# A hybrid mixer's attention values: values stationary, turned weights moving, two heads side by side

## The reference, cut to what matters

```python
scores = q @ k.T                       # (512, 512), causal
w = softmax(scores)                    # rows sum to one
attn_out[:, head] = w @ v              # (512, 64)
...
return concatenate([attn_out, yg], axis=-1) @ w_out   # 512 + 512 columns -> 1024
```

## Time and profile before

| | |
|---|---|
| median of three runs | 3214.59 us (3209.59, 3214.59, 3214.69) |
| the profiled execution's own time | 3209.03 us |
| its span | 3207.2 us |
| granted TensorE clock | 1.00 all through |
| busy: PE, PEld, DVE, ACT, POOL | 99%, 83%, 57%, 36%, 2% |
| loop iterations 3 to 9 of the first mixer | about 2130 to 2193 us |
| the same of the second mixer | about 2724 to 2787 us |

### The profile page before, as it was taken

The page is one execution under the profiler, slowest core; times in us unless marked ns, Lnnn a source line. Parts: engine busy times, 40 slices in busy tenths (PEclk is TensorE's granted clock), DMA queues, the critical chain, the costliest instruction groups (busy, mean ns, idle before and its releaser), DMA issues.

```text
span 3207.2 us, 36741 instructions
## 1 busy us (share of the span) xinstructions
PE 3190.0 (99%) x15108; PEld 2647.3 (83%) x15108; DVE 1843.9 (57%) x2667; ACT 1157.6 (36%) x1621; POOL 79.6 (2%) x110
## 2 busy tenths in 40 slices
PE   9999999999999999999999999999999999999999
PEld 8888878888888888888888888888788888878887
DVE  6664366666447664367566645987433368763332
ACT  4322254322233222263332223654322245542221
POOL 1000000000000000000000000100000010000000
PEclk9999999999999999999999999999999999999999
DMA  6443322444334443322244433211222322032322
GB/s 187 141 146 111 112 79 88 140 141 141 112 109 131 132 150 116 102 92 79 87 150 145 141 104 98 83 53 53 92 92 93 100 85 78 14 105 92 101 90 73
DMA packets 334252, 339.83 MB, mean 106 GB/s; under 512 B 12422, under 2 KB 329128, under 8 KB 334088
## 3 DMA queue, kind: packets, MB, share of 16 engines
q1 hardware_dynamic: 332128, 333.80, 32.7%
q0 software_dynamic: 1728, 3.62, 0.5%
q10 hardware_dynamic: 232, 0.06, 0.0%
HBM read 335.36 MB, written 2.10 MB: 105 GB/s over the span
## 4 chain that ended last, share of the span: by engine, by line
PE 96%; DVE 2%; ACT 1%; issue 0%; POOL 0%; DVEq 0%; POOLq 0%
PE ps L135 94%; PE ps L138 3%; DVE hl L108 1%; DVE T L108 0%; DVE wl L100 0%; ACT hh L95 0%; DVE x L100 0%; DVE ar L100 0%; DVE T L100 0%; ACT L95 0%; DVE acc L108 0%; DVE acc L100 0%; DVE x L108 0%; ACT ar L95 0%; ACT wh L95 0%
## 5 line engine op out<-in xcount | busy, mean ns | idle before, releaser
L135 PE MATMUL ps<-hh,wl 128*128 128x512 f32 x2760 | 1086.0, 393 | 2.3 <-ACT hh L95 1.5
L135 PE MATMUL ps<-hh,wh 128*128 128x512 f32 x2760 | 1075.4, 390 | 0.0
L135 PE MATMUL ps<-hl,wh 128*128 128x512 f32 x2760 | 1074.3, 389 | 0.0
L100 DVE TENSOR_TENSOR wl<-raw,wh 128x1024 fp32r<-128x1024 f32 (+3 forms) x549 | 654.3, 1193 | 696.2 <-ACT wh L95 695.8
L95 ACT ACTIVATE wh<-raw 128x1024 fp32r<-128x1024 f32 (+3 forms) x549 | 561.2, 1024 | 488.0 <-PE ps L135 487.9
L135 PEld LDWEIGHTS ps<-hh,wl 128*128 128x128 f32 x2760 | 518.2, 188 | 114.0 <-issue 5.9
L135 PEld LDWEIGHTS ps<-hh,wh 128*128 128x128 f32 x2760 | 518.1, 188 | 109.6
L135 PEld LDWEIGHTS ps<-hl,wh 128*128 128x128 f32 x2760 | 518.6, 188 | 104.7 <-issue 0.4
L135 PE MATMUL ps<-uh,wl 128*128 128x512 f32 x1056 | 412.2, 390 | 0.0
L135 PE MATMUL ps<-uh,wh 128*128 128x512 f32 x1056 | 411.1, 389 | 0.0
L135 PE MATMUL ps<-ul,wh 128*128 128x512 f32 x1056 | 410.9, 389 | 0.0
(11 more groups left out here) (239 smaller groups left out, 2668.9 us busy)
## 6 DMA issues: line engine op xcount, KB each, us to landing
raw<-in_ffn_w SPq DMA_DIRECT2D x119, 1024.0 KB, 5.3
raw<-in_w_ada SPq DMA_DIRECT2D x48, 1024.0 KB, 5.2
raw<-in_w_gate_up SPq DMA_DIRECT2D x44, 1024.0 KB, 5.0
raw<-in_m_w_in SPq DMA_DIRECT2D x26, 1024.0 KB, 5.4
raw<-in_w_down SPq DMA_DIRECT2D x16, 1024.0 KB, 5.1
raw<-in_ffn_w SPq DMA_DIRECT2D x16, 768.0 KB, 4.3
raw<-in_w_in SPq DMA_DIRECT2D x12, 1024.0 KB, 5.3
raw<-in_m_w_out SPq DMA_DIRECT2D x8, 1024.0 KB, 5.1
```

What stands on the lines that cost most here:

```text
L100: return self.issue(lambda e: e.tensor_tensor(out, a, b, op))
L135: return self.issue(lambda e: e.matmul(out, l, r, start=start, stop=stop, skip_group_check=True))
```

## The change

Values: heads 2j and 2j+1 are done together in one bank, once in two iterations. 64 columns of v are stationary and a row of PT (512, 384, 256, 128 columns for key block 0 to 3) is moving; head 2j writes partitions 0 to 63 of the bank and head 2j+1 partitions 64 to 127. The result has value columns along the partitions and tokens along the row. TensorE calls `values(j)` in iterations 3, 5, 7 and 9, between the first `between()` and `turn`.

Reciprocals: after the reciprocal DVE copies it, spread over 64 columns, into half of `A(12 + j)`. Behind the values of a pair TensorE transposes that tile (four transposes, one more bank, key `share`), ACT copies the result back to `A(12 + j)` (ahead of its copies for `turn`), and DVE multiplies the bank `val` by it in one 128x512 operation, at the end of its iteration as before.

Behind the loop the 16 transposes are gone; ACT and DVE split `A(12..15)` directly. The order of the parts becomes 0, 1, 4, 2, 5, 3, 6, 7. Two waits of ACT and DVE are changed to the new keys.

```diff
@@ TensorE
-                def values(hd):
-                    b = banks.take((s, "val", hd))
+                def values(j):
+                    heads = (2 * j, 2 * j + 1)
+                    b = banks.take((s, "val", j))
                     pe.wait_ge(*left_of((s, "v", 3)))
-                    for k in (0, 1, 2):
-                        pe.wait_ge(*left_of((s, "pt", hd, k)))
+                    for hd in heads:
+                        for k in (0, 1, 2):
+                            pe.wait_ge(*left_of((s, "pt", hd, k)))
+                    for k in range(4):
+                        for h, hd in enumerate(heads):
+                            done = pe.mm(b[64 * h:64 * h + 64, 128 * k:S], vt[:, k, 64 * hd:64 * hd + 64], PT(hd, k)[:, 0:S - 128 * k],
+                                         k == 0, k == 3)
+                    done.then_inc(formed, (s, "val", j))
+                    b = banks.take((s, "share", j))
+                    pe.wait_ge(worked, (s, "share", 2 * j + 1))
                     for q in range(4):
-                        for k in range(q + 1):
-                            done = pe.mm(b[:, 64 * q:64 * q + 64], PT(hd, k)[:, 128 * (q - k):128 * (q - k) + 128],
-                                         vt[:, k, 64 * hd:64 * hd + 64], k == 0, k == q)
-                    done.then_inc(formed, (s, "val", hd))
+                        done = pe.tr(b[:, 128 * q:128 * q + 128], A(12 + j)[:, 128 * q:128 * q + 128], ident[:, :])
+                    done.then_inc(formed, (s, "share", j))
...
                     between()
+                    if hd > 2 and hd % 2:
+                        values((hd - 3) // 2)
                     if 0 < hd < 9:
                         turn(hd - 1)
                     between()
-                    if hd > 1:
-                        values(hd - 2)
                 while next(ssd, 0):
                     pass
-                for j in range(4):
-                    b = banks.take((s, "cat", j), freed=(lo_part, (s, "c", j)))
-                    pe.wait_ge(*left_of((s, "val", 7)))
-                    for q in range(4):
-                        done = pe.tr(b[:, 128 * q:128 * q + 128], A(12 + q)[:, 128 * j:128 * j + 128], ident[:, :])
-                    done.then_inc(formed, (s, "cat", j))
@@ ACT, in the loop ahead of turn
+                    if hd > 2 and hd % 2:
+                        key = (s, "share", (hd - 3) // 2)
+                        act.wait_ge(formed, key)
+                        act.f(A(12 + (hd - 3) // 2), ps(key)[:, :], ACT.Copy).then_inc(left(key), key)
@@ ACT, behind the loop
-                        act.wait_ge(formed, (s, "cat", j))
-                        part((s, "c", j), ps((s, "cat", j))[:, :], ch[:, j, :])
+                        act.wait_ge(*left_of((s, "val", j)))
+                        act.wait_ge(formed, (s, "val", 3))
+                        part((s, "c", j), A(12 + j), ch[:, j, :])
@@ DVE, turn(hd)
-                    dve.recip(m[:, 4:8], m[:, 4:8]).then_inc(worked, (s, "share", hd))
+                    dve.recip(m[:, 4:8], m[:, 4:8]).then_inc(worked, (s, "recip", hd))
+                    dve.own()
+                    dve.copy(A(12 + hd // 2).rearrange("p (q h n) -> p q h n", q=4, h=2)[:, :, hd % 2, :],
+                             m[:, 4:8].unsqueeze(2).to_broadcast([128, 4, 64])).then_inc(worked, (s, "share", hd))
@@ DVE
-                def values(hd):
-                    m = t8[hd % 3]
-                    key = (s, "val", hd)
+                def values(j):
+                    key = (s, "val", j)
                     dve.wait_ge(formed, key)
-                    dve.wait_ge(worked, (s, "share", hd))
-                    dve.tt(A(12, 4)[:, :, 64 * hd:64 * hd + 64], ps(key)[:, 0:256].rearrange(tok4, b=4),
-                           m[:, 4:8].unsqueeze(2).to_broadcast([128, 4, 64]), MUL).then_inc(left(key), key)
+                    dve.wait_ge(*left_of((s, "share", j)))
+                    dve.tt(A(12 + j), ps(key)[:, :], A(12 + j), MUL).then_inc(left(key), key)
...
                     between()
-                    if hd > 1:
-                        values(hd - 2)
+                    if hd > 2 and hd % 2:
+                        values((hd - 3) // 2)
```

More of the change, by code:

```diff
@@ L1237, in mix2 @@
                     between()
-                    if hd > 1:
-                        values(hd - 2)
                 while next(ssd, 0):
                     pass
-                for j in range(4):
-                    b = banks.take((s, "cat", j), freed=(lo_part, (s, "c", j)))
-                    pe.wait_ge(*left_of((s, "val", 7)))
-                    for q in range(4):
-                        done = pe.tr(b[:, 128 * q:128 * q + 128], A(12 + q)[:, 128 * j:128 * j + 128], ident[:, :])
-                    done.then_inc(formed, (s, "cat", j))
                 pe.wait_ge(pooled, (s, "v8", 1))
                 along((s, "al", 1), sm[:, 4:8])
-                begin(s, [("out", 0), ("out", 1)], ch, cl, (s, "c"), (0, 4, 1, 5, 2, 3, 6, 7))
+                begin(s, [("out", 0), ("out", 1)], ch, cl, (s, "c"), (0, 1, 4, 2, 5, 3, 6, 7))
                 out_product(s, nxt, False)
@@ L1844, in scores @@
                         if hd > 2:
-                            act.wait_ge(*left_of((s, "val", hd - 3)))
+                            act.wait_ge(worked, (s, "share", hd - 3))
                         b = ps((s, "sc", hd, 0 if q == 2 else q))
@@ L1859, in turn @@
                         if hd > 1:
-                            act.wait_ge(formed, (s, "val", hd - 2))
+                            act.wait_ge(formed, (s, "val", hd // 2 - 1))
                         act.f(PT(hd, k), ps(key)[:, 0:512 - 128 * k], ACT.Copy).then_inc(left(key), key)
@@ L1956, in mix2 @@
                     pass
-                for k in (0, 4, 1, 5, 2, 3, 6, 7):
+                for k in (0, 1, 4, 2, 5, 3, 6, 7):
                     j = k % 4
                     if k < 4:
-                        act.wait_ge(formed, (s, "cat", j))
-                        part((s, "c", j), ps((s, "cat", j))[:, :], ch[:, j, :])
+                        act.wait_ge(*left_of((s, "val", j)))
+                        act.wait_ge(formed, (s, "val", 3))
+                        part((s, "c", j), A(12 + j), ch[:, j, :])
                     else:
@@ L2877, in turn @@
                     dve.wait_ge(*left_of((s, "sc", hd, 1)))
-                    dve.recip(m[:, 4:8], m[:, 4:8]).then_inc(worked, (s, "share", hd))
+                    dve.recip(m[:, 4:8], m[:, 4:8]).then_inc(worked, (s, "recip", hd))
+                    dve.own()
+                    dve.copy(A(12 + hd // 2).rearrange("p (q h n) -> p q h n", q=4, h=2)[:, :, hd % 2, :],
+                             m[:, 4:8].unsqueeze(2).to_broadcast([128, 4, 64])).then_inc(worked, (s, "share", hd))
                     dve.wait_ge(formed, (s, "pt", hd, 3))
                     if hd > 1:
-                        dve.wait_ge(formed, (s, "val", hd - 2))
+                        dve.wait_ge(formed, (s, "val", hd // 2 - 1))
                     dve.copy(PT(hd, 1), ps(key)[:, :]).then_inc(left(key), key)
-                def values(hd):
-                    m = t8[hd % 3]
-                    key = (s, "val", hd)
+                def values(j):
+                    key = (s, "val", j)
                     dve.wait_ge(formed, key)
-                    dve.wait_ge(worked, (s, "share", hd))
-                    dve.tt(A(12, 4)[:, :, 64 * hd:64 * hd + 64], ps(key)[:, 0:256].rearrange(tok4, b=4),
-                           m[:, 4:8].unsqueeze(2).to_broadcast([128, 4, 64]), MUL).then_inc(left(key), key)
+                    dve.wait_ge(*left_of((s, "share", j)))
+                    dve.tt(A(12 + j), ps(key)[:, :], A(12 + j), MUL).then_inc(left(key), key)
                 def states():
@@ L3060, in mix2 @@
                     between()
-                    if hd > 1:
-                        values(hd - 2)
+                    if hd > 2 and hd % 2:
+                        values((hd - 3) // 2)
                 while next(ssd, 0):
                     pass
-                for k in (0, 4, 1, 5, 2, 3, 6, 7):
+                for k in (0, 1, 4, 2, 5, 3, 6, 7):
                     j = k % 4
                     if k < 4:
-                        dve.wait_ge(formed, (s, "cat", j))
-                        part((s, "c", j), ps((s, "cat", j))[:, :], ch[:, j, :], cl[:, j, :]).then_inc(lo_part, (s, "c", j))
+                        dve.wait_ge(formed, (s, "val", 3))
+                        part((s, "c", j), A(12 + j), ch[:, j, :], cl[:, j, :]).then_inc(lo_part, (s, "c", j))
                     else:
@@ L3072, in mix2 @@
                             scaled(j)
-                        dve.wait_ge(formed, (s, "cat", 3))
+                        dve.wait_ge(lo_part, (s, "c", j))
                         part((s, "c", k), A(16 + j), ch[:, k, :], cl[:, k, :]).then_inc(lo_part, (s, "c", k))
```

## The result

The changed kernel takes 3245.26 us (median of five runs, 3237.65 to 3245.59), the kernel before 3214.07 in the same comparison (3209.59 to 3214.69): a ratio of 1.0096, 95% interval 1.0085 to 1.0106. It is slower by 31 us. I had forecast slower, 3225 us, with a range up to 3240: the direction was right, and the time lies above the range.

What follows compares the result with a forecast made beforehand. TensorE, 99% busy, was taken as the bound, just hiding the DVE, ACT, DVE chain. Twice 6.7 us of lateness gave 13.5 more: 3222.5 on the profiled execution, 3228.1 on the median, middle 3225; range 3212 to 3240.

Steps and rivals of the forecast that it cites:

- TensorE's work: Values, share and final transposes: a pair costs 2.88 us in place of 4.46; 8.1 us less in a layer.
- third rival: Values of a pair: two wide moving operands don't run side by side, a pair costs 4.6 us; 3236 us, chance 0.12.
- DVE and ACT: Added work in the loop: +0.45 us a head on DVE, about 0.48 a pair for ACT's extra copy.
- A to D: First mixer's chain: scores 4 late by 2.6 us, scores 6 by 5.3, `y` of frames(3) by 7.3, output product by 6.7.
- 1.6 us for POOL at the end: Ahead of the last `along`: about 1.6 us of TensorE idle, as nothing hides POOL's power any more.
- From there all is as before: Behind the first output product nothing else changes; the second mixer repeats the first, twice 6.7 is 13.5 us more.
- B: Scores 6 in the first mixer: start at 2166.9 instead of 2161.64, late by 5.3 us.
- C: `y` of frames(3) in the first mixer: DVE's multiply ends at 2191.3, `y` started at 2184.04, late by 7.3 us.
- D: End of the first mixer: output product starts at 2202.5 instead of 2195.77, late by 6.7 us.
- The banks come free in time: Rival on the loop's `val` banks: emptied within about 2.8 us, TensorE's own work sets the end; 3198 us, chance 0.15.
- other side: Rival: banks empty in time, TensorE's own work sets the end, -7 us per layer; 3198 us, chance 0.15.
- Half of it: Rival: scores 4 and 6 late, but DVE catches up in iterations 6 to 8; +1.8 us a layer, 3215 us, chance 0.13.

Runs made afterwards that it cites:

- e2_early: The changed kernel, with DVE multiplying a pair's values ahead of its SSD step in iterations 3, 5 and 7 instead of behind it: 3215.90 us, ratio 1.0007.
- e3_cover: The changed kernel, with TensorE repeating instructions (same results) ahead of its long waits, no wait of other engines shortened: 3224.70 us, ratio 1.0034.
- e5_front: The changed kernel, with a pair's values at the head of iterations 3, 5 and 7 on TensorE, ACT and DVE, end unchanged: 3212.13 us, ratio 0.9998.
- e6_both: The changed kernel with values moved as in e5_front, and the end reordered (last turned weights earlier, last `along` inside the output product): 3199.63 us, ratio 0.9963.
- e7_old_tail: The kernel before, with only the end reordered: `turn(7)` earlier, last `along` behind the output product's third part: 3218.60 us, ratio 1.0022.
- e8_one_by_one: The changed kernel, with the values' loops exchanged so that one head's four blocks precede the other's: 3240.45 us in one run.

## Why the prediction was wrong, point by point

**TensorE's work: right.** 2.30 us for a pair against 2.44 forecast; the entry into the half-width form and the way out cost 0.12 and not 0.29. The third rival, no pairing, is out by this row. The Trainium skill, "TensorEngine Tiling (Array Packing)", names twofold column tiling for this swap in its section Performance Considerations and a factor of up to two in its section Overview; the trace agrees, with 4.46 / 2.30 = 1.94. Performance Considerations also says that tiling doesn't speed up the emptying of PSUM. TensorE did come to wait for the emptying (7.9 us), but not because it takes long: DVE's multiply is 0.68 us, and e2_early took the waits away by its place in DVE's order alone.

**DVE and ACT: near.** From the reciprocal to the spread copy 0.21, from the copy to the next start 0.21 (2166.14, 2166.35, 2166.56). That is 0.42 where it was 0.09 before, so 0.33 more a head and not 0.45; ACT's extra copy made a row of 1.04 us one of 1.48, 0.44 against 0.48.

**A to D: right at full clock.** Forecast, then e3_cover, then the changed kernel: scores 4 at 2143.3, 2144.02, 2143.70; scores 6 at 2166.9, 2167.61, 2170.61; `y` of frames(3) at 2191.3, 2191.82, 2196.49; output product at 2202.5, 2202.36, 2207.38. The first column is met within 0.7 us by e3_cover. The changed kernel leaves it behind scores 4, where its clock falls, and not before. The whole kernel: 3222.5 forecast on the profiled execution's time, 3222.88 in e3_cover. That this is so close is in part luck: 1.7 us of it is e3_cover's one stretch at half clock, and the second output product is 12.7 us later than before (2802.10) where the steps give 13.4. The 1.6 us for POOL at the end are 1.61.

**The step that failed** is the sum behind the steps: "From there all is as before", and with it that every duration in B, C and D is one taken at full clock. The front's own table says 1.00 all through, and I carried it over to a kernel into which I had just put waits of 2.5 to 4 us. The clock costs 3237.65 - 3222.88 = 14.8 us, more than the 13.9 (3222.88 - 3209.03) that the waits leave over once the saved work is taken off them. In the forecast this term stood at nothing, without a reason. The 34 us at half clock which the changed kernel has more than e3_cover are 17 us of TensorE's time; that some 2 of them fell into waits would give the 14.8, but isn't shown. Of the 20 us between 3225 and the median, 15.2 are there in the profiled execution (3237.65 against 3222.5); the other 5.1 are that the median lies 7.6 above this execution, where my middle of two levels had allowed 2.5. That is the clock again: 0.991 to 0.992 in the other four runs against 0.994 in this one. In the range the term is missing too: its upper end came from prices and rivals, all at full clock.

**The rivals.** "The banks come free in time" stated its own condition, `val` emptied within 2.8 us; e2_early and e5_front meet it and land at 3215.9 and 3212.1, 14 to 18 us above the 3198 that I had for that case. Its sum left out the waits for ACT at the end (1.7 us in both) and the clock there. e6_both comes near 3198, with 3199.63, but it also takes out POOL's 1.6 us, which the rival's sum had kept. So the other side is real, with a smaller gain than I gave it, and it isn't this kernel. "Half of it" did not come: in e3_cover the lateness does not shrink behind B (6.0 at scores 6, 7.8 at `y`).

Not settled: why the clock falls in e7_old_tail, and why waits of 2.3 and 2.9 us bring no fall in the first mixer of e8_one_by_one; and how much of e6_both's gain hangs on the mended end together with the pairs, since the end alone, on the kernel before, gains nothing.

## What to carry to other kernels

When a change shortens the bound engine's program, follow the rotation of its buffers: find for each bank who empties it and how many takings lie between, and put the emptying instruction ahead of other work on its engine; one such move in DVE's order was worth 29 us here, the change itself 16 at best by the sum and 12.6 in e6_both. And where a forecast puts waits of 2 us or more on a TensorE that ran without any, price what follows them at the lower clock as well as at the full one: here that doubled the loss, though not every such wait brings the fall. A test for this is cheap: fill the waits with repeated instructions, and see whether the kernel gets faster.

## What the runs showed of the hardware

TensorE's clock fell to half (1.2 of 2.4 GHz) behind single waits of 2.3 and 3.5 us, and around those of 1.2 and 1.6 us at the end of the loop, for 3 to 7 us each time, in a program that is 99% busy over the span. The same wait doesn't always do it: no fall began behind the 2.02 us at 2196.49, and one did behind the same 2.02 us in the second mixer (2806.9), and those of 2.31 and 2.89 us in e8_one_by_one brought none. The Trainium skill, "TensorE: Matmul & The Clock Gate", Part 1, describes a gate with these two levels that goes by how busy the engine has lately been; this trace agrees, with 0.58 over 2143.7 to 2150.0 behind 1.00. But it also fell where hardly any idle time lay ahead (0.15 us in e7_old_tail), and 46 transposes in a row with no idle time kept it at 1.00 in e3_cover.

The kernel before is not free of it either. Among the runs of it beside e6_both, those at 3208.8 to 3209.5 us have a mean clock of 1.000, those at 3213.8 to 3214.9 one of 0.998: the spread of 5.5 us between the runs goes with the clock (0.002 x 3207 = 6.4 us, of a clock rounded to 0.001).

Two fp32 matmuls with 64 stationary columns and up to 512 moving ones share TensorE (2.30 us for 16 instructions, whose 40 steps of 0.109 would be 4.36 one after the other). With all instructions of one half ahead of those of the other the same 16 take 3.86, so they mostly don't.
